# A fused encoder step: weight loads issued by ScalarE, a second plain pair, and three reorderings

## The reference

```
h  = rms_norm(x)
[u | v_g | q | k | v | g] = h @ w_in                       # 1024 x 5632
A  = gelu(u) * (W_s * layer_norm(gelu(v_g)) + b_s)         # in chunks of 128 rows
B  = sliding-window attention, 16 heads, 4 kv heads, with ALiBi and sinks
x  = x + (sigmoid(g_A) * (A @ w_pa) + sigmoid(g_B) * (B @ w_pb)) @ w_o
x  = x + (gelu(causal_conv3(h2 @ w_up_gate)) * (h2 @ w_up_val)) @ w_down
y  = rms_norm(x)
```

## Time and profile before

| | |
|---|---|
| time, three runs | 1746.06 us median (1744.42 to 1748.01) |
| profiled execution | 1745.02 us, its span 1743.2 us |
| instructions | 31424 |
| mean granted TensorE clock | 0.988 |
| busy: TensorE / weight load / VectorE / ScalarE / GpSimd | 96% / 93% / 61% / 38% / 20% |
| bytes moved | 209.40 MB, nearly all from SP's queue |

### The profile page before, as it was taken

The page is one execution under the profiler, slowest core; times in us unless marked ns, Lnnn a source line. Parts: engine busy times, 40 slices in busy tenths (PEclk is TensorE's granted clock), DMA queues, the critical chain, the costliest instruction groups (busy, mean ns, idle before and its releaser), DMA issues. The chain is left out here.

```text
span 1743.2 us, 31424 instructions
## 1 busy us (share of the span) xinstructions
PE 1679.1 (96%) x12614; PEld 1625.8 (93%) x12614; DVE 1055.9 (61%) x1828; ACT 661.5 (38%) x1232; POOL 346.7 (20%) x321
## 2 busy tenths in 40 slices
PE   6799999999999897999999999999999999999997
PEld 6798888888889897999999999999999998999997
DVE  6746565565646673242242877777777776666665
ACT  6435444454544333342343544333334332111112
POOL 2321121212113440001222522222222220000001
PEclk9999999999999998999999999999999999999999
DMA  8343434243335756465444122222222226222122
GB/s 250 115 154 107 129 97 133 84 138 95 104 117 174 202 163 220 128 220 161 137 141 143 51 68 82 75 75 75 75 76 87 85 79 238 95 93 97 66 74 104
DMA packets 240579, 209.40 MB, mean 120 GB/s; under 512 B 24759, under 2 KB 197619, under 8 KB 240435
## 3 DMA queue, kind: packets, MB, share of 16 engines
q1 hardware_dynamic: 240206, 207.32, 37.6%
q10 hardware_dynamic: 229, 0.08, 0.0%
HBM read 141.91 MB, written 65.45 MB: 119 GB/s over the span
## 5 line engine op out<-in xcount | busy, mean ns | idle before, releaser
L2053 PE MATMUL ps<-op_hi,w_hi 128*128 128x272 f32 x3248 | 688.8, 293 | 25.9 <-DVE quad L1619 9.1
L2053 PE MATMUL ps<-op_hi,w_lo 128*128 128x272 f32 x3248 | 672.8, 289 | 0.0
L2053 PE MATMUL ps<-op_lo,w_hi 128*128 128x272 f32 x3248 | 672.3, 288 | 0.0
L2053 PEld LDWEIGHTS ps<-op_hi,w_hi 128*128 128x128 f32 x3248 | 510.7, 189 | 53.0 <-issue 48.0
L2053 PEld LDWEIGHTS ps<-op_lo,w_hi 128*128 128x128 f32 x3248 | 512.5, 189 | 0.0
L2053 PEld LDWEIGHTS ps<-op_hi,w_lo 128*128 128x128 f32 x3248 | 509.9, 189 | 0.0
L1512 DVE TENSOR_TENSOR w_lo<-raw,w_hi 128x512 fp32r<-128x512 f32 x224 | 163.6, 746 | 202.9 <-ACT w_hi L1151 202.9
L1151 ACT ACTIVATE w_hi<-raw 128x512 fp32r<-128x512 f32 x224 | 134.8, 626 | 153.6 <-PE ps L2053 128.8
L1958 DVE TENSOR_TENSOR xy<-ps,xy 128x728 f32<-128x728 f32 (+1 forms) x176 | 119.4, 720 | 95.8 <-PE ps L2254 95.8
L994 POOL TENSOR_TENSOR w_f<-raw 128x512 f32<-128x512 f32 x42 | 62.6, 1491 | 566.9 <-PE ps L2053 553.3
L1222 ACT ACTIVATE u<-ps 128x544 f32<-128x544 f32 x84 | 52.2, 621 | 189.0 <-PE ps L2053 189.0
(11 more groups left out here) (168 smaller groups left out, 1657.8 us busy)
## 6 DMA issues: line engine op xcount, KB each, us to landing
in_spill<-quad SPq DMA_DIRECT2D x88, 272.0 KB, 2.2
raw<-in_w_in_dram SPq DMA_DIRECT2D x44, 512.0 KB, 5.4
raw<-in_w_up_dram SPq DMA_DIRECT2D x44, 512.0 KB, 5.0
g_spill<-value_out SPq DMA_DIRECT2D x22, 544.0 KB, 2.7
g_in<-g_spill SPq DMA_DIRECT2D x11, 1088.0 KB, 5.8
d_raw<-in_w_down_dram SPq DMA_DIRECT2D x22, 512.0 KB, 3.4
q_now<-in_spill SPq DMA_DIRECT2D x36, 128.0 KB, 2.4
gate_q<-in_spill SPq DMA_DIRECT2D x16, 272.0 KB, 6.6
```

The source lines that it names most:

```text
L2053: last = pe.matmul(out[:, h, 0:HB], (w_hi, w_lo)[a][place][:, j, :], (op_hi, op_lo)[b][at][:, j, HB * h:HB * h + HB], start=fresh and j == ...
```

## The change

- The weight load moves from SP's program to ScalarE's: pair p + 1's weights are issued in pair p at product 0, j = 3 (in a seven-product pair behind a plain one, at product 1, j = 2). Only pair 0's stay with SP.
- Pair 1 becomes plain. `lead(g)` gives the last of the plain pairs at the head of a group; waits that were written for pair 1 now go by it. Operands 2, 5 and 4 of the first group are made in pairs 1 and 2. Copies of pairs 1 to 21 out of PSUM that are written by ScalarE wait for the store of the quadrant before.
- Raw operands: two pairs ahead of groups 1 and 2, SP loads r21 alone; the first operand, r12 and r22 follow one pair ahead, and (group 1) the four gates behind them.
- For groups 3 and 4, part "b" of operand 1 is made in the pair before, and part "b" of operand 7 comes one tile earlier; the normalisation of the third quadrant of pairs 31 to 33 is done in the pair itself.
- `row_factor` comes after the third weight sum, `norm_rows(0)` and `factor_in(0)` one tile later.
- The last tile's `value_scale` and `gated_value` come after the first and the second down addition.

The diff, without lines that only define `lead`, its callers, the moved body of `load_weights` and contexts:

```diff
-PLAIN = (0,) + tuple(range(PB, UP)) + (UP,)
+PLAIN = (0, 1) + tuple(range(PB, UP)) + (UP,)
...
@@ SP, base
-                    if p + 1 < NPAIR:
-                        load_weights(p + 1)
...
@@ SP, background
-                        load_operands(g, src)
+                        load_operands(g, src, (1,))
+                    if p == FIRST_PAIR[g] - 1 and (n, j) == (1, 0):
+                        load_first_operand(g, src)
+                        load_operands(g, src, (0, 2))
                         if g == 1:
                             for q in order_of(PB):
                                 load_gate_b(PB, q)
-                    if p == FIRST_PAIR[g] - 1 and (n, j) == (1, 0):
-                        load_first_operand(g, src)
...
@@ GpSimd, background
-                if p == UP and (n, j) == (4, 0):
-                    row_factor()
...
                         weight_sum(p + 1, places.index((n, j)))
+                if p == UP and (n, j) == (5, 0):
+                    row_factor()
...
@@ ScalarE, operands
                             todo = {(1, 2): ((0, "a"),), (2, 2): ((1, "a"),), (3, 2): ((0, "b"),), (5, 1): ((7, "a"),),
-                                    (5, 2): ((3, "a"),)}.get((n, j), ())
+                                    (5, 2): ((3, "a"),), (6, 2): ((1, "b"),)}.get((n, j), ())
...
-                            todo = {(3, 0): ((3, "w"),), (5, 0): ((2, "w"),)}.get((n, j), ())
+                            todo = {(3, 0): ((3, "w"),)}.get((n, j), ())
...
-                            todo = {(0, 1): ((1, "b"),), (0, 3): ((7, "b"),), (1, 0): ((6, "a"), (6, "b")), (2, 1): ((3, "b"),),
+                            todo = {(0, 2): ((7, "b"),), (1, 0): ((6, "a"), (6, "b")), (2, 1): ((3, "b"),),
...
                     if (p, g) == (1, 0):
-                        todo = {(0, 2): ((5, "w"),), (0, 3): ((4, "w"),)}.get((n, j), ())
+                        todo = {(5, 0): ((2, "w"),), (6, 1): ((5, "w"),)}.get((n, j), ())
+                    if (p, g) == (2, 0):
+                        todo = {(0, 1): ((4, "w"),)}.get((n, j), ())
...
@@ ScalarE, background
-                if stage(p) == "out" and j == 1 and n in ((2, 5) if plain(p) else (2, 5, 6)):
+                if stage(p) == "out" and j == 1 and n in ((2, 5) if p == OUT else (2, 5, 6)):
...
                 if OUT < p <= UP and (n, j) == (0, 1):
-                    if plain(p - 1):
+                    if p - 1 == OUT:
                         normed(4 * (p - 1 - OUT) + 2)
...
@@ ScalarE, main loop
+                        if (k, j) == ((1, 2) if not plain(p) and plain(p - 1) else (0, 3)) and p + 1 < NPAIR:
+                            load_weights(act, p + 1)
                         for m in ahead(p, k, j, False):
                             weight_hi(p + 1, m)
...
@@ VectorE, operands
-                            lows = {(1, 0): ((3, "w"),), (5, 2): ((2, "w"),)}
+                            lows = {(4, 0): ((3, "w"),)}
...
                     if (p, g) == (1, 0):
-                        lows = {(0, 2): ((5, "w"),), (1, 0): ((4, "w"),)}
+                        lows = {(5, 2): ((2, "w"),), (6, 2): ((5, "w"),)}
+                    if (p, g) == (2, 0):
+                        lows = {(0, 3): ((4, "w"),)}
...
@@ VectorE, down stage
             taps(FT - 1)
-            value_scale(FT - 1)
-            gated_value(FT - 1)
...
                         last.then_inc(s_added, 1)
+                        if n == 0:
+                            value_scale(FT - 1)
+                        if n == 1:
+                            gated_value(FT - 1)
...
@@ TensorE, background
-                if (p, n, j) == (UP + 1, 0, 0):
+                if (p, n, j) == (UP + 1, 0, 1):
                     norm_rows(0)
```

More of the change, by code:

```diff
@@ L147, with lead @@
 END_PAIR = (PB, PA, OUT, UP, NPAIR)
+def lead(g):
+    p = FIRST_PAIR[g]
+    while p + 1 < END_PAIR[g] and plain(p + 1):
+        p += 1
+    return p
 def summed(g):
@@ L527, in weights_of, with load_weights @@
             return k_tiles(w_up), (p - UP) * P, FF + (p - UP) * P
+        def load_weights(engine, p):
+            if p:
+                engine.wait_ge(s_w, LOWS_BEFORE[p])
+            view, c1, c2 = weights_of(p)
+            for c, c0 in enumerate((c1, c2)):
+                engine.dma_start(raw[:, c], view[:, :, c0:c0 + P]).then_inc(s_raw, 16)
         def place(t, i, q):
@@ L605, in load_x @@
                 sp.dma_start(xt[0:rows_of(n), n % XT, :], token_rows(n)).then_inc(s_x_in[n % XT], 16)
[L607 to L612, removed]
             def store_xt(n):
@@ L621, in _ @@
                 load_x(n)
-            load_weights(0)
+            load_weights(sp, 0)
             for n in range(5, NT):
@@ L647, in stored, with load_operands @@
                     sp.wait_ge(s_q_out[q], 16 * store_count(q, p + 1))
-            def load_operands(g, src):
+            def load_operands(g, src, some):
                 for i, (dst, k, half) in enumerate(((r12, 0, 1), (r21, 1, 0), (r22, 1, 1))):
+                    if i not in some:
+                        continue
                     sp.dma_start(dst[:], src.rearrange("(j k) p t -> k p j t", k=2)[k][:, :, half * QT:half * QT + QT])\
@@ L1155, in operand_hi @@
                 if g or n == 2:
-                    act.wait_ge(s_product, place_freed(first if n == op_place(g, 7) else first - 1, at))
+                    act.wait_ge(s_product, place_freed(lead(g) if n == op_place(g, 7) else first - 1, at))
                 if g == 0:
@@ L1212, in copied @@
                 if plain(p - 1):
-                    act.wait_ge(s_comb, 4 * (p - 1) if p > 1 else 1)
+                    act.wait_ge(s_comb, 4 * (p - 1))
                 else:
                     act.wait_ge(s_comb, comb_count(p - 1, (Q11, Q12, Q21)[i]))
-                if p == 1:
+                if p == lead(0) + 1:
                     act.wait_ge(s_xts_out[1], 16 * (NT - 4))
@@ L1280, in free_place @@
                 kind = stage(p)
-                if kind == "pb":
+                if kind in ("in", "pb") and p:
                     act.wait_ge(s_q_out[q], 16 * store_count(q, p))
@@ L1866, in background @@
                 if f == 0:
-                    if (n, j) == (0, 1):
+                    if (n, j) == (0, 2):
                         factor_in(0)
@@ L2006, in product_waits @@
                 g = generation(p)
-                if p == FIRST_PAIR[g] or p == FIRST_PAIR[g] + 1:
+                if p <= lead(g) + 1:
                     pe.wait_ge(s_op, op_count(g, operand))
```

6 lines of the change are left out of this document (3 added, 3 removed).

## The result

| | before | after |
|---|---|---|
| time, median (range), four runs each | 1746.72 us (1744.42 to 1748.01) | 1731.38 us (1729.97 to 1734.17) |
| ratio, 95% interval | | 0.9916 (0.9898 to 0.9933) |
| profiled execution, its span | 1745.02, 1743.2 us | 1731.90, 1730.1 us |
| busy TensorE / VectorE / ScalarE / GpSimd | 96 / 61 / 38 / 20% | 97 / 60 / 38 / 19% |

Faster by 0.84%, 15.3 us. The prediction was 1720.0 in a range of 1709 to 1733, so the sign and the range held, while the forecast of 26 us was too large by some 11.

The account below looks back on a forecast made before the run. TensorE, busy 1679.1 of 1743.2 us, was taken as the bound, so only matmuls and its standstills count. -4.0 + 1.2 - 6.4 - 11.0 - 2.0 - 3.3 = -25.5 gave 1720 us against the median, range 1709 to 1733.

Parts of the forecast that it names:

- Two plain pairs: Start of the kernel: one product more, but two waits shrink or go and one comes; -4.0 us (-7 to +1).
- Weights from ScalarE: Weight loads of 55 pairs leave SP's queue: gMLP stage -6.4 us, attention +1.2, up stage 0.
- 4.8 + 1.6: gMLP stage near 585: 4.8 of the 5.11 us wait go, and 1.6 of slow restart behind it.
- Up stage: ScalarE's weight issue costs 0.99 us within a cover of 1.25 us: 0, with 0.2 us to spare.
- rival B: Up stage: ScalarE's issue does not fit in its cover, about twenty times; +13 us, 1733, chance 0.10.
- Raw operands ahead of the gates: Boundary of pair 22: weights and operands land in time, so the 9.1 us wait goes; -11.0 us (-8 to -11.5).
- the slow restart: Matmuls running slowly behind a long TensorE wait; at pair 22 estimated at 1.9 us, to go with the wait.
- about 1 MB in 3.5 us: Landing rate taken at pair 22, putting the weights in at 661 us, needed at 662.5.
- Up boundary: Moved operand parts, normalisation and row factor: the 1.53 us wait goes; -2.0 us for all boundaries together (-5 to +2).
- Down additions: Start of the down stage: the first addition runs earlier and frees TensorE at 1459.2; -3.3 us (-2 to -5).
- Rival A: Queue change saves only issue time, the store lands no sooner; -1.2 instead of -6.4 us, 1725, chance 0.15.
- C: Rival: start and up boundary both at their bad bounds, +1 and +2 instead of -4 and -2; 1729, chance 0.07.

Follow-up runs that it names:

- e10: The changed kernel with only one plain pair first and operands 2, 5 and 4 of the first group at their old places; 1732.17 us.
- e9: The changed kernel with the weights of pairs 18 to 21 issued by SP again, behind the store of the gMLP tile; 1730.33 us.
- e4: The changed kernel with all weight loads issued by SP at their old places; 1729.12 us.
- e1: The changed kernel with pair 22's weights issued by SP again, right ahead of the first raw operand; 1723.66 us.
- e5: The kernel before, with the weight loads issued by ScalarE and nothing else changed; 1737.41 us.
- e6: The changed kernel with everything around the output and up boundaries as before; 1729.42 us.
- e2: The changed kernel, but SP waits until pair 22's weights have landed before it issues the first operand, r12, r22 and the gates; 1726.67 us.
- e11: The changed kernel with scale and gating of the last tile ahead of the first down addition again; 1735.39 us.
- e12: The changed kernel with the edits of e1, e6 and e9 together; 1721.00 us.

## Why the prediction was right and wrong

1. **Two plain pairs: right.** Forecast -4.0, measured -2.9 at pair 3. Operand 6's wait became 1.17 (about 1), the m1c wait went, and 2.49 came at the value transposes (3.0), behind the chain that was written out. What is missing is the clock ahead of these waits: at the start of the kernel TensorE has 6.0 us of matmuls at 0.50 after, 3.8 before. In the kernels with two plain pairs the gain spreads from 1.6 to 3.8, mostly by that and by the clock at 93. Not seen: half of it is given back at later waits (e10).
2. **Weights from ScalarE: the gMLP stage right in sign, undersized.** -8.6 against -6.4; the term that was mis-sized is the size of the whole stage, since the 4.8 + 1.6 counted one of its tiles (3.3 + 1.7 measured) and the "small waits on tile loads around it", 3.1 measured, were put only into the bound. The reason given, the store no longer behind the weights, holds, but not "the queue": e9 has it without one. Attention: +1.2 expected, 0.0 measured. Up stage: 0, right; rival B falls. ScalarE's queue issues beside its own activation, see below.
3. **Raw operands ahead of the gates: the step that failed.** -11.0 expected, +0.6 measured, and it is 11.6 of the 12.4 us by which the sum of -25.5 missed the -13.1 of the spans. The order itself is worth 9.8 (e4), the slow restart was 1.9 as estimated (e1). What failed is the landing time: "about 1 MB in 3.5 us" treated the two queues as one line, in which who is issued first lands first. With the weights in a queue of their own they shared every turn with pieces four times their size and took 17.7 us instead of 7. The text even said that the share of a second queue was not shown, in part 2, and then used a price without it in part 3. The bounds of -8 to -11.5 had no side for it. (The 5.9 MB of that price are 6.7 in the trace of before, which makes 3.1 us for 1 MB; it would have changed nothing.)
4. **Up boundary: sign wrong.** -2.0 expected, +2.8 measured, outside the bound of +2. The shift of VectorE's queue by 2.2 us was seen, and that the square sum hangs on it; what failed is "there I find the same time as before" and the chain behind the first product: GpSimd's large sum hangs on the same add, starts 3.0 us later, and with it come its weight sums and the weight difference that TensorE waits for. That "the chain ahead starts later by some 3 us" was in the text, but not priced. Of the 2.8 us 1.4 are standstill and 1.2 half clock.
5. **Down additions: right.** -3.3 against -3.6, the wait 1.44.

The stages as measured, -2.9 + 0.0 - 8.6 + 0.6 - 0.2 (24 to 33) + 2.8 + 0.0 - 3.6 - 1.2, make the -13.1 of the spans. Without the miss of part 3 the sum would have given 1731 against the profiled run, but that is luck: the other errors, +1.1, -1.2, -2.2, +4.8, -0.3, -0.2 and -1.2, nearly cancel. That 1731.4 lies in the range is luck too: its upper part was there for rivals A, B and C, and none of them had weights that land late. Rival A fails in its price and in its reason, since the store landed in 4.6 us instead of 6.1; it was right in that no second queue is needed. C's half on the up boundary came true.

## What to carry to other kernels

In one queue the load that was issued first landed first here; in two queues they share by pieces, so a load with short rows loses most of its bandwidth to long rows beside it. Move a load to another engine's queue where nothing large runs against it; where it must land first, keep it ahead of the others in the same queue. Before crediting a second queue, try the same load later in the first one. And look at the granted clock behind every standstill before a difference of 1 or 2 us is put down to an edit.

## What the runs showed of the hardware

- Two queues divide the engines by pieces, not by bytes: with work in both, 882 pieces of one and 885 of the other were moved (after), 1518 and 1518 (e5). 505-byte pieces against 2050 took 14.3 us for 512 KB in the median, against pieces of mostly 544 bytes 9.4, and 8.4 in one queue ahead of them. The Trainium skill, "DMA: Bandwidth & Descriptors", section "Queues, rings and completion order", states that each engine takes turns between queues packet by packet, a packet being a group of some 9 to 17 descriptors. These runs agree in the equal shares; whether a turn is one piece or several they do not tell.
- ScalarE issues DMAs while it computes: the couple of 1.01 us lies wholly beside the convolution start, and pairs 37 to 55 take 378.8 us as before. It had been counted as taking 0.99 us out of a cover of 1.25.

```profile
1006.20 1.30 ACT L1367 ACTIVATE conv<-a_ext,consts,conv_w 128x1090 f32<-128x1090 f32 x1 [2.92 <-DVE a_ext L1792]
1006.22 1.01 ACTq L543 DMA_DIRECT2D raw<-in_w_up_dram  x2
```

- GpSimd's and VectorE's sums of 2176 columns, started within 0.6 us of each other, took 5.43 and 7.11 us; in e6, where VectorE's came behind, 4.88 and 3.51. A VectorE difference of 544 columns, 0.73 us elsewhere, took 3.41 (e6) and 5.20 us (e2) beside GpSimd's sum.
- TensorE's granted clock fell to 0.50 behind or in some standstills and not behind others of the same length: behind the same 2.49 us wait at 93 us in e11 and e12, and not in the other nine kernels that have it. At pair 22 a wait of 2.21 us (e1) left it at 1.00, one of 9.71 (after) had it at 0.50 for 4.3 us of matmuls.
